# Quarter stage of a hybrid decoder layer: norm roots and reciprocals on three columns of 86 tokens, scalings ahead of late sums, squares in two rings

## The reference, cut to what matters

```python
z  = merged @ w_out                                   # 1024 x 1024
x1 = x + z * rsqrt(mean(z * z) + eps) * g_post_mix
h2 = x1 * rsqrt(mean(x1 * x1) + eps) * g_pre_mlp
f  = square(relu(h2 @ w_ff1))                         # 1024 x 4096
y  = x1 + rmsnorm(f @ w_ff2, g_post_mlp)
```

## Time and profile before

| | us |
|---|---|
| median of three runs (lowest, highest) | 2011.98 (2010.7, 2014.7) |
| the profiled execution, its own time | 2014.58 |
| its span, from the first to the last instruction | 2012.8 |
| TensorE busy | 1957.8 (97%) |
| VectorE, ScalarE, POOL busy | 903.7, 621.5, 896.5 |
| mean granted clock of TensorE | 0.989 |

### The profile page before, as it was taken

One profiled execution on the slowest core, in us unless ns is written; L12 is line 12 of the kernel. 1 busy time (PEld: TensorE's weight loads), 2 busy tenths in 40 slices (PEclk: granted clock), 3 DMA queues, 4 the chain that ended last, 5 costly groups with the idle time before them and its releaser, 6 DMA issues.

```text
span 2012.8 us, 33480 instructions
## 1 busy us (share of the span) xinstructions
PE 1957.8 (97%) x13077; PEld 1908.2 (95%) x13077; DVE 903.7 (45%) x1966; ACT 621.5 (31%) x1184; POOL 896.5 (45%) x533
## 2 busy tenths in 40 slices
PE   8999999999999999999989999799999999999996
PEld 6999999999999999999969999699999999999996
DVE  6504550154403552054577743888676740111126
ACT  6312211122012220122146546644444453212121
POOL 7453233333333233423442237579777764443412
PEclk9999999999999999999999999899999999999999
DMA  5312331134211331123654354513323252223412
GB/s 190 105 43 85 136 110 43 43 115 141 74 53 58 136 136 43 43 89 141 225 175 147 123 158 129 137 46 124 124 88 125 77 211 87 103 85 105 147 53 85
DMA packets 89289, 218.22 MB, mean 108 GB/s; under 512 B 7721, under 2 KB 40745, under 8 KB 88793
## 3 DMA queue, kind: packets, MB, share of 16 engines
q1 hardware_dynamic: 78784, 192.48, 28.6%
q10 hardware_dynamic: 10392, 24.14, 3.4%
HBM read 162.93 MB, written 53.66 MB: 108 GB/s over the span
## 4 chain that ended last, share of the span: by engine, by line
PE 88%; DVE 5%; issue 2%; ACT 2%; POOL 2%; DMA 0%; DVEq 0%; SPq 0%; ACTq 0%; POOLq 0%
PE bank L892 78%; PE bank L1041 1%; PE bank L1044 1%; PE bank L1235 1%; PE bank L1033 1%; PE bank L996 1%; PE bank L1039 1%; PE bank L1133 1%; POOL w_lo L698 1%; DMA w_raw<-w_stream 0%; ACT P_sb L1437 0%; POOL h_lo L713 0%; DVE acc L2074 0%; DVE gates L2071 0%; DVE acc L1763 0%
## 5 line engine op out<-in xcount | busy, mean ns | idle before, releaser
L892 PE MATMUL bank<-h_hi,w_hi 128*128 128x344 f32 (+1 forms) x2048 | 651.1, 318 | 2.4 <-POOL w_lo L698 2.2
L892 PE MATMUL bank<-h_lo,w_hi 128*128 128x344 f32 (+1 forms) x2048 | 637.7, 311 | 0.0
L892 PE MATMUL bank<-h_hi,w_lo 128*128 128x344 f32 (+1 forms) x2048 | 636.0, 311 | 0.0
L702 POOL TENSOR_TENSOR w_hi<-w_raw,ones 128x1024 fp32r<-128x1024 f32 x77 | 147.4, 1914 | 628.1 <-PE bank L892 628.1
L892 PEld LDWEIGHTS bank<-h_hi,w_hi 128*128 128x128 f32 x2048 | 387.4, 189 | 7.1 <-issue 3.5
L892 PEld LDWEIGHTS bank<-h_hi,w_lo 128*128 128x128 f32 x2048 | 387.2, 189 | 0.9
L892 PEld LDWEIGHTS bank<-h_lo,w_hi 128*128 128x128 f32 x2048 | 387.1, 189 | 0.0
L704 POOL TENSOR_TENSOR w_lo<-w_raw,w_hi 128x1024 fp32r<-128x1024 f32 x77 | 185.7, 2412 | 6.1
L2241 DVE TENSOR_TENSOR acc<-acc,bank 128x344 f32<-128x344 f32 x72 | 36.9, 513 | 292.0 <-PE bank L892 292.0
L1268 ACT ACTIVATE side_t<-bank 128x344 f32<-128x344 f32 x96 | 44.0, 459 | 284.3 <-PE bank L892 284.3
L1763 DVE SCALAR_TENSOR_TENSOR acc<-acc,rstd 128x258 f32<-128x258 f32 x128 | 126.7, 1032 | 0.1
(11 more groups left out here) (434 smaller groups left out, 4407.7 us busy)
## 6 DMA issues: line engine op xcount, KB each, us to landing
w_raw<-w_stream SPq DMA_DIRECT2D x113, 512.0 KB, 3.7
d_side<-side_t ACTq DMA_DIRECT2D x32, 516.0 KB, 2.6
f_raw<-d_f SPq DMA_DIRECT2D x24, 516.0 KB, 4.5
gates<-d_side SPq DMA_DIRECT2D x24, 344.0 KB, 4.1
d_f<-sq SPq DMA_DIRECT2D x16, 516.0 KB, 3.3
dC<-stC SPq DMA_DIRECT2D x32, 256.0 KB, 3.7
qkb<-d_qk SPq DMA_DIRECT2D x32, 256.0 KB, 4.0
o_C_s<-dC SPq DMA_DIRECT2D x32, 256.0 KB, 2.0
```

Source lines behind the costliest of these rows:

```text
L702: pool.tensor_tensor(w_hi[:, slot, :], w_raw[:, slot, :], ones[:, 0:1].to_broadcast([P, 1024]), ALU.mult).then_inc(s_hi_made, 1)
L892: last = pe.matmul(out, st, mv, start=i == 0, stop=i == n - 1)
```

## The change

In the quarter stage a sum over partitions is now made the other way round: the 258 tokens of a quarter are loaded as weights in three parts of 86 and multiplied with one column of ones, so that three columns of 86 rows come out in place of 258 columns of 128 equal rows. Root and reciprocal run on 86 x 3 elements. VectorE multiplies the identity by each column, which gives three diagonal blocks side by side (86 x 258), and TensorE spreads them over all partitions by a product with ones. The spreads of z stand after product 17 and after tile 4; the four of x1 stand after tile 13, and ScalarE copies them to `rstd0`. The means of x1 move: the first of h = 1 from tile 4 to tile 8, the eight squares of s = 1, h = 0 from tile 6 to tile 10, those of h = 1 from tile 10 to tile 13. The squares of s = 1, h = 0 go to a second ring of eight (`x1_sq2`), so they don't wait for the sums that read the first. On VectorE `x1_sums(1)` goes from between the two scalings of s = 1 to behind `combine(0, 5)`, `x1_add_last` goes ahead of the low halves, and the combines of s = 0 are dealt out between the operands of s = 1. The core of the diff:

```diff
+B86 = 86
...
+        tok_col = sb("tok_col", [P, 18])
...
+        x1_sq2 = z_sq + [rstd0b[:, qt[e]] for e in range(4)]
+        z_col = [tok_col[0:B86, 3 * h:3 * h + 3] for h in range(2)]
+        x1_col = [[tok_col[0:B86, 6 + 6 * s_ + 3 * h:9 + 6 * s_ + 3 * h] for h in range(2)] for s_ in range(2)]
+        x1_row_bank = [[bank[3], bank[6]], [bank[7], bank[3]]]
+        def diag_of(t):
+            return t[0:B86, :].rearrange("p (j t) -> p j t", j=3)
...
 TensorE
+            def columns(out, parts):
+                for j in range(3):
+                    for i, t in enumerate(parts):
+                        last = pe.matmul(out[0:B86, j:j + 1], t[:, B86 * j:B86 * (j + 1)], ones[:, 0:1],
+                                         start=i == 0, stop=i == len(parts) - 1)
+                return last
             def z_mean(s, h):
                 ...
-                pe.matmul(b_mean[h][:, 0:Q4], ones[:, :], z_sum[h], start=True, stop=True).then_inc(s_z_ssq, 1)
+                columns(b_mean[h], [z_sum[h]]).then_inc(s_z_ssq, 1)
+            def z_spread(s, h):
+                pe.wait_ge(s_z_scaled, 18 * s + h + 1)
+                pe.matmul(b_mean[h][:, 0:Q4], ones[0:B86, :], z_std[h][0:B86, :], start=True, stop=True).then_inc(s_z_ssq, 1)
+            def x1_mean_first(h):
+                pe.wait_ge(s_x1_sum, 7 * (h + 1))
+                columns((bank[6], bank[3])[h], [x1_std[h]]).then_inc(s_x1_ssq, 1)
+            def x1_spread(s, h):
+                pe.wait_ge(s_x1_sum, 14 + 2 * s + h + 1)
+                pe.wait_ge(s_x1_std, 5 if s and h else 4)
+                pe.matmul(x1_row_bank[s][h][:, 0:Q4], ones[0:B86, :], rstd0[0:B86, qt[2 * h + s]], start=True, stop=True)\
+                    .then_inc(s_x1_ssq, 1)
 ... (z products)
+                if c == 17:
+                    z_spread(0, 0)
+                    z_spread(0, 1)
                 if c == 26:
-                    ... (one 258-column product of x1_std[0])
+                    x1_mean_first(0)
 ... (tiles; banks 3, 6, 7)
-                    pe.wait_ge(s_x1_std, 4)
-                    pe.wait_ge(s_z_scaled, 32)
+                    pe.wait_ge(s_x1_std, 8)
+                    pe.wait_ge(s_z_scaled, 36)
 ... (after tile t)
                 elif t == 4:
-                    ... (one 258-column product of x1_std[1], waits for s_x1_sum 14)
-                elif t in (6, 10):
-                    ... (eight 258-column products of x1_sq[k], h = 0 after tile 6, h = 1 after tile 10)
+                    z_spread(1, 0)
+                    z_spread(1, 1)
+                elif t == 8:
+                    x1_mean_first(1)
+                elif t == 10:
+                    pe.wait_ge(s_x1_ready_dve, 4)
+                    pe.wait_ge(s_xg, 24)
+                    columns(bank[6], x1_sq2).then_inc(s_x1_ssq, 1)
+                elif t == 13:
+                    pe.wait_ge(s_x1_std, 2)
+                    pe.wait_ge(s_x1_sq, 8)
+                    columns(bank[3], x1_sq).then_inc(s_x1_ssq, 1)
+                    for s in range(2):
+                        for h in range(2):
+                            x1_spread(s, h)
...
 ScalarE (roots on 86 x 3 elements; h=0 squares of s=1 into the second ring)
-                root(z_std[h], b_mean[h][:, 0:Q4], s_z_ssq, 2 * s + h + 1, s_z_std)
+                root(z_col[h], b_mean[h][0:B86, 0:3], s_z_ssq, 4 * s + h + 1, s_z_std)
...
-                            act.wait_ge(s_x1_sum, 14)
-                        square = x1_sq[k]
+                            act.wait_ge(s_z_ssq, 8)
+                        square = x1_sq2[k]
... (x1_last_square)
-                    act.wait_ge(s_x1_ssq, 2 + k + 1)
+                    if k == 0:
+                        act.wait_ge(s_x1_sum, 14)
...
+            def x1_rows(s, h):
+                act.wait_ge(s_x1_ssq, 4 + 2 * s + h + 1)
+                act.activation(rstd0[:, qt[2 * h + s]], x1_row_bank[s][h][:, 0:Q4], ACT.Copy).then_inc(s_x1_std, 1)
...
             copy_c(0, 1, 0)
-            x1_root(0, 1)
             copy_c(0, 2, 0)
             ...
             b_high(1, 0)
-            x1_last_square(range(4))
             b_high(1, 1)
-            x1_last_square(range(4, 8))
             wc_high(7)
             b_high(1, 2)
+            x1_last_square(range(4))
             b_high(1, 3)
+            x1_last_square(range(4, 8))
+            x1_root(0, 1)
             wc_high(8)
             ...
             b_high(1, 6)
+            x1_root(1, 0)
             copy_c(0, 1, 1)
             copy_c(0, 2, 1)
             wc_high(9)
             wc_high(10)
-            x1_root(1, 0)
             x1_root(1, 1)
+            (four x1_rows, in order of s and h)
...
 VectorE
+            def diagonal3(out, col):
+                step(dve.reciprocal(col, col))
+                return dve.tensor_tensor(diag_of(out), ident[0:B86, 0:B86].unsqueeze(1).to_broadcast([B86, 3, B86]),
+                                         col.unsqueeze(2).to_broadcast([B86, 3, B86]), ALU.mult)
             def z_inverse(s, h):
                 dve.wait_ge(s_z_std, 2 * s + h + 1)
-                step(dve.reciprocal(b_mean[h][:, 0:Q4], z_std[h]))
+                diagonal3(z_std[h], z_col[h]).then_inc(s_z_scaled, 1)
             def z_scale(s, h, ks):
+                dve.wait_ge(s_z_ssq, 4 * s + 3 + h)
...
             def x1_inverse(s, h):
                 dve.wait_ge(s_x1_std, 2 * s + h + 1)
-                step(dve.reciprocal(q, q))
+                diagonal3(rstd0[:, qt[2 * h + s]], x1_col[s][h]).then_inc(s_x1_sum, 1)
... (x1_add_last: scratch bank[6] for bank[3]; b_add(1, 6) also waits for s_x1_sq 8; combine "u" of pair 0 for s_x1_std 4 + 2 s + half + 1)
             z_inverse(0, 0)
+            z_inverse(0, 1)
             z_scale(0, 0, range(8))
-            z_inverse(0, 1)
             z_scale(0, 1, range(8))
             ...
             z_inverse(1, 0)
+            z_inverse(1, 1)
             z_scale(1, 0, range(8))
-            x1_sums(1)
-            z_inverse(1, 1)
             z_scale(1, 1, range(4))
+            x1_add_last()
             b_low(0, 5)
+            combine(0, 1, "dfe", (0,))
             b_low(0, 6)
-            combine(0, 1, "dfe", (0,))
             combine(0, 2, "dfe", (0,))
-            x1_add_last()
-            for p in range(3, 7):
-                combine(0, p, "dfe", (0,))
             b_add(1, 0)
             b_add(1, 1)
+            combine(0, 3, "dfe", (0,))
             b_low(1, 0)
+            combine(0, 4, "dfe", (0,))
             b_add(1, 3)
             b_low(1, 1)
+            combine(0, 5, "dfe", (0,))
+            x1_sums(1)
             b_low(1, 2)
+            combine(0, 6, "dfe", (0,))
             b_low(1, 3)
             ...
             (four x1_inverse, then combine(0, p, "u") for s = 0 and s = 1; until now two inverses ahead of each s)
```

More of the change, by code:

```diff
@@ L371, in hybrid_layer, with z_scales @@
         x1_std = [rstd0[:, qt[2 * h]] for h in range(2)]
+        x1_sq2 = z_sq + [rstd0b[:, qt[e]] for e in range(4)]
[4 more added lines that the diff above has]
+            return t[0:B86, :].rearrange("p (j t) -> p j t", j=3)
+        def z_scales(s, h, k):
+            return 18 * s + 2 + 8 * h + k + 1
         f_st = [[sq0[:, 0, :], sq0[:, 1, :]], [rstd0b[:, :], zsq[:, :, :].rearrange("p g t -> p (g t)")]]
@@ L1172, in _ @@
                     z_mean(0, 1)
+                if c == 17:
+                    z_spread(0, 0)
+                    z_spread(0, 1)
                 if c == 26:
-                    pe.wait_ge(s_x1_sum, 7)
-                    pe.matmul(b_mean[0][:, 0:Q4], ones[:, :], x1_std[0], start=True, stop=True).then_inc(s_x1_ssq, 1)
+                    x1_mean_first(0)
             for t in range(14 * PAIRS):
@@ L1203, in _ @@
                 elif t == 4:
-                    pe.wait_ge(s_x1_sum, 14)
-                    pe.matmul(bank[3][:, 0:Q4], ones[:, :], x1_std[1], start=True, stop=True).then_inc(s_x1_ssq, 1)
-                elif t in (6, 10):
[L1207 to L1217, removed]
+                    z_spread(1, 0)
[13 more added lines that the diff above has]
+                            x1_spread(s, h)
             def ff2_group(u, g, bank_of=None):
@@ L1490, in root @@
                 act.wait_ge(summed, count)
-                act.activation(dst, src, ACT.Sqrt, scale=1.0 / D, bias=eps[:, 0:1]).then_inc(made, 1)
+                act.activation(dst, src, ACT.Sqrt, scale=1.0 / D, bias=eps[0:dst.shape[0], 0:1]).then_inc(made, 1)
             def z_root(s, h):
-                root(z_std[h], b_mean[h][:, 0:Q4], s_z_ssq, 2 * s + h + 1, s_z_std)
+                root(z_col[h], b_mean[h][0:B86, 0:3], s_z_ssq, 4 * s + h + 1, s_z_std)
             def wc_high(n):
@@ L1554, in x1_root @@
             def x1_root(s, h):
[L1555 to L1558, removed]
+                root(x1_col[s][h], (bank[6], bank[3])[h][0:B86, 0:3], s_x1_ssq, 2 * s + h + 1, s_x1_std)
+            def x1_rows(s, h):
+                act.wait_ge(s_x1_ssq, 4 + 2 * s + h + 1)
```

(15 more changed lines are left out.)

5 lines of the change are left out of this document (2 added, 3 removed).

## The result

The changed kernel takes 2023.11 us (median of five, 2021.9 to 2025.96) against 2014.56 in the same rounds (2010.7 to 2014.96): ratio 1.005, 95% interval 1.0038 to 1.0061. It is slower by 8.6 us by the medians and 10 by the ratio (interval 8 to 12). I had forecast slower, 2017.1, at most 2021.5; the time is outside the range. Of the 6.0 us between 2017.1 and 2023.11, 2.6 come from the base: I added to 2011.98, the median of three, and the kernel before has 2014.56 here. The change itself costs 8.6 where I had 5.15. Among the executions of the experiments three single executions took 3848 to 4979 us, one of them of the kernel before; the ratios leave them out. What came about is the mechanism of the rival to which I gave 0.18, with 2022.0: one-column products don't keep the clock up.

What follows compares the result with a forecast made beforehand. TensorE was taken as the bound almost everywhere, with four stops in the quarter stage. Chain -0.9, tail +6.1, tile 22 -2.85 and clock +2.85 gave +5.15 us on 2011.98: 2017.1, range 2009.0 to 2021.5.

Steps and rivals of the forecast that it cites:

- The clock: Stops between 1301 and 1313 us slow tile 10 (+1.2) and half the first column block (+1.7): 2.85 us.
- third rival: Tiles 10 to 12 and column blocks: one-column products don't keep the clock up; +10 us, 2022.0; chance 0.18.
- upper bound of 8.5: Highest value, in us, set for the clock term, if the column blocks keep the clock low.
- Prices: Costs of the new small operations: column record 0.071 us, inverse 0.63 for 1.78, root about 0.25.
- The claim that the form saves TensorE nothing: Column means cost as much as 258-column means (3.4 against 3.3 us over eight tiles); every spread, 0.41, is extra.
- First half: Up to tile 4: s=0 means and spreads cost TensorE 0.82 us, POOL's hold 0.4; tile 4 ends 1.2 later.
- The hold by POOL: VectorE's diagonal products near 1236 us held by POOL's instructions: TensorE waits up to 1.1 us, taken as 0.4.
- VectorE's chain: Second half, tiles 5 to 13: tile 7 gains 5.5 us, of which 0.9 are left at tile 13.
- The tail: Behind tile 13: column products, root, four spreads and row copies without cover, 6.1 us before tile 14.
- Sum without the clock: Net at full clock: chain -0.9, tail +6.1, vanished wait at tile 22 -2.85, giving +2.3 us.
- Full clock throughout: Rival: clock stays at 2.4 GHz, so only the tail counts; +2.3 us, 2014.3; chance 0.24.
- the parting of VectorE and POOL: Rival: VectorE's chain escapes POOL's holds, tile 13 ends before 1321.8; -0.35 us, 2011.6; chance 0.22.

Runs made afterwards that it cites:

- experiment 6: Changed kernel with 80 columns of ones and x1 spreads behind tiles 14 to 17: 2014.45 us, ratio 1.0006; with idle TensorE time also filled: 2014.16, 1.001.
- experiment 2: Changed kernel with the four x1 spreads moved behind tiles 14 to 17, tiles 14 and 15 waiting for three roots only: 2017.36 us, ratio 1.0024.

## Why the prediction was wrong, step by step

**The clock: the step that failed.** I put 2.85 us into the sum for it: tile 10 slow (1.2) and half of the first block (1.7). The mechanism behind that was a clock brought down by TensorE's stops. In the profile tiles 9 and 10 were slow (5.07 us to 1314.40), but experiment 6 shows no price for that, and the first block was nearly at full speed. What I put at nothing came from the blocks themselves, busy as they were. Against the kernel with 80 columns, from tile 9 to tile 22: first block 0.3, tiles 11 to 13 6.96 for 4.40, second block to the first spread 5.49 for 4.28, spreads to tile 14 4.30 for 2.50, tile 14 to 22 14.24 for 11.56. Sum 8.6 us in the traces, 6.6 by the medians. My third rival had this mechanism, 7.7 us of clock and +10 in all; its places were partly others (the first block slow throughout, the spreads and tiles 14 to 17 not counted), so that its 2022.0 comes so near 2023.11 is in part luck, the more so as it stood on the lower base. The upper bound of 8.5 that I set on the clock term doesn't come out of that rival's own sum. I gave the rival 0.18 because its only row mixed transposes with one-column products and was one fall in eight such stretches (3.46 us once, 2.03 seven times). But those stretches were 1.7 us long and the new blocks 3.4 by my own price, which I wrote down and did not let weigh. The rule that activity releases the clock (the Trainium skill, TensorE: Matmul & The Clock Gate, What's actually happening) was the better guide. Busy time by the records can't stand for that activity: it was 10.00 of 10.00 us in the steady loop with the clock down (one column) and with the clock up (80 columns).

**Prices.** The column record was 0.075 at full clock (32 records from 1314.40 to 1316.80) where I took 0.071; 0.02 and 0.106 were the bounds. The inverse was as computed: 0.17 and 0.42. A root took 0.24 to 0.26 against 0.25. (The 0.43 that I cite from the earlier trace rows stands in the earlier trace rows.) The claim that the form saves TensorE nothing held.

**First half.** 1.9 us by the end of tile 4, where I had 1.2. The hold by POOL was there, 1.50 for a product that takes 0.42 alone, ending 0.3 us behind an instruction of POOL that had begun before it; VectorE in the changed kernel:

```profile
...
1232.08 1.50 DVE L2133 TENSOR_TENSOR rstd0b<-ident,tok_col 86x258 f32<-86x258 f32 x1
1233.51 0.16 DVE L2132 RECIPROCAL tok_col<-tok_col 86x3 f32<-86x3 f32 x1
1233.70 0.42 DVE L2133 TENSOR_TENSOR rstd0b<-ident,tok_col 86x258 f32<-86x258 f32 x1
```

TensorE waited only 0.32 for it; the rest is the column means and the spreads, dearer than I had them by some 0.7.

**VectorE's chain.** Counted from product 16, tile 5 came 1.1 us later than before, forecast 0.3. Tile 7 came 5.1 us earlier, forecast 5.5; tile 9 1.4, forecast 1.9. VectorE did wait for the s=1 spread, 1.18 us. That tile 10 would be reached late through ScalarE's order was right too, with waits of 0.41 and 0.40 in place of one. The end of tile 13 was forecast 0.9 earlier; at full clock (80 columns) it was 0.9 later, in the changed kernel 3.6 later.

**The tail.** 6.1 us forecast at full clock; 6.8 with 80 columns, 9.8 in the changed kernel. That it has no cover is shown by experiment 2, where tile 14 comes 3.6 behind the end of tile 13 and not 9.8. Tile 22 stopped waiting, as forecast.

**Sum without the clock.** I had +2.3 us; the kernel with 80 columns is 2.6 over before by the medians, 3.8 by the ratio (4.7 in its trace). So the rest of the ledger held, with errors of a microsecond or two, and the clock term was the one that was badly mis-sized.

**The rivals.** Full clock throughout (0.24) and the parting of VectorE and POOL (0.22) did not come: the low half of operand 4 still took 2.30 us, where that of operand 5 took 1.22, and tile 13 did not end early. The range ended 1.6 us short, and even at 0.5 below the rival's own time, because I gave little weight to a mechanism that I had priced; the base, 2.6 us higher in these rounds, is the other part.

## What to carry to other kernels

A reduction that turns data into weights and moves one column saved TensorE nothing here (3.77 us for 48 records against 3.65 for the 16 records of 258 columns), and it let the clock fall while the engine looked busy. Move more columns as long as the block takes no longer (80 were free here), or keep the wide product. Before work is taken from the engine that waits in chain, ask which engine stands idle beside it: eight plain products in a gap of 10 us were worth more here than eight cheap reciprocals. When a mechanism is priced and a row, however mixed, speaks for it, its price belongs in the range.

## What the runs showed of the hardware

With 86 columns of weights, 48 records took 3.77 to 3.83 us at the full clock whether one or 80 columns were moved. Busy time in the records doesn't tell the clock: at 10.00 of 10.00 us busy the granted clock was 0.66 to 0.83 after a one-column block and 1.00 after one of 80 columns. A root of 86 x 3 elements takes ScalarE 0.24 to 0.26 us, about half of the 0.48 for 128 x 258.
